# First weight tile rounded on VectorE, and a quarter of x transposed after two matrix products: a two-block fp32 network on one core

## What is computed

```python
def rmsnorm(x, g):
    xf = x.astype(jnp.float32)
    y = xf * lax.rsqrt(jnp.mean(xf * xf, axis=-1, keepdims=True) + NORM_EPS) * g.astype(jnp.float32)
    return y.astype(x.dtype)

def first_block(x, positions, norm_mix, w_in, ...):
    ...
        h = rmsnorm(x, norm_mix[layer])
        (q, kc, vc, ks, vs, kw, vw, nsa_g, rq, rk, rv, rg, gate_a, gate_b) = jnp.split(
            h @ w_in[layer], offsets, axis=-1)
        ...
```

## Time and profile before

| | us |
|---|---|
| median of 3 runs | 949.09 |
| lowest, highest | 949.04, 949.36 |
| the profiled execution, its own time | 948.88 |
| its span in the profile | 947.1 |
| busy in the span: PE, PEld | 940.2, 868.0 |
| busy in the span: DVE, ACT, POOL | 709.4, 563.5, 134.6 |

### The profile page before, as it was taken

The page is one execution under the profiler, slowest core; times in us unless marked ns, Lnnn a source line. Parts: engine busy times, 40 slices in busy tenths (PEclk is TensorE's granted clock), DMA queues, the critical chain, the costliest instruction groups (busy, mean ns, idle before and its releaser), DMA issues.

```text
span 947.1 us, 17052 instructions
## 1 busy us (share of the span) xinstructions
PE 940.2 (99%) x6904; PEld 868.0 (92%) x6904; DVE 709.4 (75%) x947; ACT 563.5 (59%) x861; POOL 134.6 (14%) x186
## 2 busy tenths in 40 slices
PE   9999999999999999999999999999999999999997
PEld 7877999989999999989988999998998899999997
DVE  5768875779778887878876787776667468777777
ACT  6577564557666566666865674545455455455544
POOL 3000001005223220404000001100000032121211
PEclk9999999999999999999999999999999999999999
DMA  9964447545666566656565365555655346565661
GB/s 316 307 219 150 133 112 179 176 159 185 199 198 199 182 197 200 185 158 198 148 186 170 99 204 175 176 184 172 196 163 168 122 156 192 181 197 188 194 207 67
DMA packets 133807, 170.39 MB, mean 180 GB/s; under 512 B 5824, under 2 KB 98064, under 8 KB 133728
## 3 DMA queue, kind: packets, MB, share of 16 engines
q1 hardware_dynamic: 131552, 165.08, 56.7%
q10 hardware_dynamic: 1536, 2.77, 0.8%
q0 software_dynamic: 640, 1.44, 0.7%
HBM read 168.22 MB, written 1.05 MB: 179 GB/s over the span
## 4 chain that ended last, share of the span: by engine, by line
PE 98%; DVE 1%; DMA 0%; issue 0%; POOLq 0%; ACT 0%; ACTq 0%; DVEq 0%; POOL 0%
PE ps L441 23%; PE ps L409 15%; PE ps L410 15%; PE ps L413 15%; PE ps L391 4%; PE ps L584 3%; PE ps L923 3%; PE ps L927 3%; PE ps L922 3%; PE ps L867 2%; PE ps L863 2%; PE ps L864 2%; PE ps L616 1%; PE ps L619 1%; PE ps L474 1%; PE ps L615 1%
## 5 line engine op out<-in xcount | busy, mean ns | idle before, releaser
L1814 DVE TENSOR_TENSOR parts<-raws,parts 128x1024 fp32r<-128x1024 f32 (+3 forms) x307 | 363.7, 1201 | 120.6 <-ACT parts L1244 119.7
L1244 ACT ACTIVATE parts<-raws 128x1024 fp32r<-128x1024 f32 (+3 forms) x307 | 308.5, 1028 | 120.1 <-PE ps L413 51.1
L409 PE MATMUL ps<-room_r,parts 128*128 128x256 f32 x1248 | 308.6, 281 | 0.0
L410 PE MATMUL ps<-room_r,parts 128*128 128x256 f32 x1248 | 306.4, 279 | 0.0
L409 PEld LDWEIGHTS ps<-room_r,parts 128*128 128x128 f32 x1248 | 234.3, 188 | 2.2 <-issue 0.8
L410 PEld LDWEIGHTS ps<-room_r,parts 128*128 128x128 f32 x1248 | 235.0, 188 | 1.2
L441 PE MATMUL ps<-parts,room_r 128*128 128x512 f32 (+1 forms) x960 | 225.4, 392 | 0.0
L441 PEld LDWEIGHTS ps<-parts,room_r 128*128 128x128 f32 x960 | 175.6, 188 | 40.0 <-issue 0.4
L413 PE MATMUL ps<-room_r,parts 128*128 128x256 f32 x1248 | 196.5, 279 | 0.0
L413 PEld LDWEIGHTS ps<-room_r,parts 128*128 128x128 f32 x1248 | 167.7, 188 | 0.0
L1848 DVE TENSOR_TENSOR room_r<-room,room_r 128x512 fp32r<-128x512 f32 (+2 forms) x75 | 53.6, 721 | 31.0 <-ACT room_r L1542 10.1
(11 more groups left out here) (252 smaller groups left out, 1159.1 us busy)
## 6 DMA issues: line engine op xcount, KB each, us to landing
raws<-in_w_in SPq DMA_DIRECT2D x99, 512.0 KB, 4.4
raws<-in_w_ffn_in SPq DMA_DIRECT2D x44, 512.0 KB, 4.7
raws<-in_w_up SPq DMA_DIRECT2D x32, 512.0 KB, 3.9
raws<-in_w_down SPq DMA_DIRECT2D x32, 512.0 KB, 3.8
raws<-in_w_ffn_out SPq DMA_DIRECT2D x22, 512.0 KB, 4.4
raws<-in_w_xkv SPq DMA_DIRECT2D x16, 512.0 KB, 3.9
raws<-in_w_out SPq DMA_DIRECT2D x8, 512.0 KB, 4.6
raws<-in_w_up_ssd SPq DMA_DIRECT2D x8, 512.0 KB, 5.1
```

The lines of the kernel that those rows point to most:

```text
L409: e.matmul(ps, wh, hT[0][:, k, :], start=k == 0, stop=False)
L410: e.matmul(ps, wh, hT[1][:, k, :], start=False, stop=False)
L1244: e.activation(t.h, t.raw, ACT.Copy).then_inc(s["hi"], 1)
L1814: e.tensor_tensor(t.l, t.raw, t.h.bitcast(F32), ALU.subtract).then_inc(s["lo"], 1)
```

## The change

On PE, `first_block` yields once more, behind the first two products of w0 (the rounded part of block 0 of x times the rounded part of w0). The second `x_quarter` is emitted at that point instead of ahead of the whole block, and one `idle` goes. On ACT, the rounding of w0 goes: ACT rounds the first two blocks of x at once, sets its tile counter to 1, and waits until `hi` is 1 before it rounds w1. On DVE a copy makes w0's rounded part, when w0 has landed, ahead of the rest of w0. The two banks that the block sums in are thereby taken ahead of those of the second x_quarter.

```diff
@@ first_block (PE)
                 need(s["x_even_hi"], 1)
                 for t in range(2):
                     product(w0, 0, t, 0, w0.h, True)
+                yield
                 need(s["lo"], w0.i + 1)
@@ PE, start
             idle(6)
             x_quarter(0)
-            idle(2)
-            x_quarter(1)
+            idle(1)
 
             w_in = a["w_in"][0]
             units = first_block("qkv", w_in)
+            next(units)
+            x_quarter(1)
             next(units)
@@ ACT, start
-            round_tile()
             quarter_rounded(0)
+            hi = 1
+            e.wait_ge(s["hi"], 1)
             round_tile()
             quarter_rounded(1)
             round_tile()
@@ DVE, start
+            first = tiles[0]
+            e.wait_ge(landed[first.slot], first.load)
+            e.tensor_copy(first.h, first.raw).then_inc(s["hi"], 1)
             rest_of_tile()
             quarter_rest(0)
```

## The result

| | median, us | lowest, highest | runs |
|---|---|---|---|
| before, same chips | 949.29 | 948.93, 951.47 | 19 |
| changed | 951.51 | 949.78, 952.86 | 19 |
| ratio | 1.0018 | 95% interval 1.0012 to 1.0024 | |
| changed, profiled execution | 952.86 (span 951.1) | | 1 |

The account below looks back on a forecast made before the run. PE, busy 98% of 947.1 us, was taken to bound the kernel. The profiled 948.88 less 0.05 gave 948.83; plus 0.21 to the median, 949.04, rounded to 949.0; range 948.4 to 949.6 us.

Parts of the forecast that it names:

- What bounds the kernel: PE is one long queue of matmuls, 98% of 947.1 us; only its early dummy or idle time, under 1 us, is winnable.
- The step that failed: ACT, without w0's rounding (0.63 us), starts x's first block at 4.5 to 4.9 us instead of 5.25.
- T0: Start of PE's first product, needing w0 and x's block 0 rounded: 5.2 to 5.5 us, taken as 5.3.
- The sum for PE: w2's first product due at T0 + 3.39 = 8.69 us, allowed at 8.87; a 0.32 us lead shrinks to 0.02.
- Rival B: Late first product on PE: beyond T0 = 5.62 each 0.1 us costs 0.1; 949.4 with 0.3 lateness; chance 0.09.
- the prediction's own 0.21: Median of the runs before stands 0.21 us above the profiled execution of 948.88; turns 948.83 into 949.04.
- Rival C: PE's standstill from about 5.1 to T0 drops its clock level, losing 1.5 to 1.8 us: 950.5 to 950.8; chance 0.02.
- One removed idle is worth nothing by itself: On PE, removing one idle (0.61 us of dummies) gains nothing, since PE would have waited for T0 anyway.
- DVE's copy: DVE's 128x512 copy rounding w0, extrapolated to 0.43 us, taken as 0.45; w0 rounded at 5.13 to 5.40.
- w2 as the place where the head start ends: ACT's rounding of w2 still ends at 8.82 us, so PE waits there 0.18 us, losing its earlier start.
- The gain of 0.05 us: Net saving for the whole kernel, 0.02 to 0.11 us, taken as 0.05: 948.83 in a profiled execution.
- The banks and the other half of x: Changed bank picks at three scores cost 0; x's other half lands near 8.5 and 9.1 us, before PE at 9.9.

Follow-up runs that it names:

- first profile: The changed kernel's profiled execution in the main measurement, the slowest of its 19 runs: 952.86 us.
- lower group: The faster cluster of one kernel's runs; for the changed kernel median 950.01 us (8 of 19), measured again 949.96 (7 of 11), where the profiled run took 949.96.
- PE's part alone: Kernel before plus only the extra yield, later second x_quarter and one idle less; ACT still rounds w0, no DVE copy: 951.03 us against 949.10.
- the changed kernel again: The changed kernel, unaltered, measured and profiled a second time: 950.04 us against 949.10 for the kernel before.
- upper group: Runs more than 1 us above the rest of the same kernel; 4 of 11 for the changed kernel measured again, 951.50 to 952.72 us.
- the early load: Changed kernel plus one tiny copy as ACT's first instruction, waiting only for the zeros, so the table load comes early: 949.12 us against 949.15.
- the swapped waits: Changed kernel with ACT's two waits ahead of x's first block reordered, PE's first, then the gain's: 949.10 us against 949.15.

## Why the prediction was wrong, point by point

*What bounds the kernel.* Right. PE is full from its first products to the end; what was lost in 20 us is lost at 950.

*The step that failed: "ACT ... starts on x's first block when its transposes are done, at some 4.5 to 4.9".* It costed the removed rounding as 0.63 us less on ACT and forgot what came with ACT's first activation. The table load stands at 1.74 in ACT's timeline, under the same line (1244) as the rounding that the change takes out; the stretch shown in the earlier trace rows begins at 4 us and leaves it out. With it T0, put at 5.2 to 5.5, came at 6.83 in the first profile and at 6.71 in the second. The Trainium skill ("ScalarE: Activation LUTs", section "Step-by-step: what each stage is for") says that the compiler puts the load right ahead of the activation that needs it. The traces agree, 1.74 before, 4.92 after. That the load also takes over a wait, and which one, stands on the measured rows: released by PE at 4.92, by the gain at 3.61, by w0's transfer at 5.00, in three kernels that differ in which wait is issued last. The Trainium skill ("ScalarE: Activation LUTs", section "What ACT_TABLE_LOAD costs") gives about 1.28 us for the load and 1.38 for a drain beside it; here the load takes 1.28 and the next activation starts 0.01 us behind it, so 1.28 is the price.

*The sum for PE.* Its formula was nearly right and its T0 wrong. Rival B said that from T0 = 5.62 on every 0.1 us costs 0.1. In the lower group's profile T0 is 6.71: 948.88 + 6.71 - 5.62 = 949.97, and that execution took 949.96. That close a match is partly luck: the eight transposes are 1.01 us late there and not 1.09, since the third product comes 0.90 behind the first and not 0.97, and with the prediction's own 0.21 from that execution to the median the sum gives 950.18, where the lower groups' medians are 950.01 and 949.96. B was dismissed with "T0 is at most 5.5 by the bounds above"; the bounds were worked out from ACT's and DVE's known work, and the unknown piece was not in them.

*Rival C, the lower level.* The price was right: 1.5 to 1.8 us forecast, 1.85 (PE's part alone), 1.67 (the changed kernel again) and 1.48 (the kernel before without dummies) measured between the medians of the groups. The mechanism was right in part. C let the level fall while PE stands still; in the three profiles from upper groups it had not risen yet (dummies or transposes 0.21 us apart up to the gap, the first products behind it 0.43 to 0.57) and rose late. C and B were also priced as rivals, and the upper group has both: B's late product and C's level together make the 951.5. The chance, 0.02, was the second error. It rested on the standstill of 0.34 us at 5.37 in the earlier trace rows, behind which products ran at the higher level. But the rows beside it say that the level had already risen there: the dummies at 4.76 are the ones that load in 191 ns. A gap after the rise is no evidence on a gap before it. Several of the other profiles show dummies at about 333 ns until 5.0 and later (the changed kernel, the early load, PE's part alone), so one execution was taken for all. The Trainium skill ("TensorE: Matmul & The Clock Gate", section "Part 1: The HAM clock gate"), cited beside C, says that the clock is throttled by default and that activity releases it. The traces agree in the direction: 6 of 11 runs are in the upper group when the kernel before loses its dummies.

*"One removed idle is worth nothing by itself."* Wrong for that reason: in PE's part alone the dummy is what covers the gap at the lower level (7 of 11 runs at 951 without it, 0 of 11 with it). Behind the late load one dummy is not enough (4 of 11 with both). Its 0.61 us is also misread: that is the time of both dummies in the earlier trace rows, four instructions.

*DVE's copy.* Right: 0.43 us, as extrapolated from the earlier trace rows; the changed kernel's DVE row is

```profile
4.95 0.43 DVE L2008 CAST parts<-raws 128x512 fp32r<-128x512 f32 x1 [3.96 <-DMA raws<-in_w_in]
```

*w2 as the place where the head start ends.* Its time was right: with the early load w2's rounding ends at 8.80 (forecast 8.82). That PE waits there shows with the swapped waits (0.40 us); with the early load the head start was gone before w2, by the later first product (5.46 where 5.3 was taken) and its lower level. The gain of 0.05 us that was expected is neither shown nor refuted: 949.12 against 949.15 lies far within the interval (0.9992 to 1.0010).

*The banks and the other half of x.* Right; the shift between the two traces is the same at 22 and at 754 us, and behind the first products no row of PE up to 22 us waits for a transfer.

## What to carry to other kernels

When ACT's first instruction is moved or removed, look for its table load in the trace and see what that will wait for afterwards: give it an early activation of its own, or, of two waits, issue last the one that is over first. Dummy products that look free in one profile may be what keeps PE at work until its clock level rises; judge them by the spread of many runs, and read the level from the distances of products and the lengths of weight loads, not from the granted clock of a whole span. A bound on a start time has to hold every instruction on that engine's queue, so read the queue from its beginning.

## What was not expected of the hardware

An ACT table load holds back the activation behind it by 1.28 us and can itself be held back by a semaphore that the activation was meant to wait for. The level of PE's clock in the first 15 us differs from execution to execution of one program: its products were 0.233 us apart, but for the first one behind a wait or transposes, from 6.7 on in one execution of the changed kernel, and fourteen of them took 5.54 us in another, which ended 2.9 us later.
